# Expert stage of a transformer kernel: earlier first rows, later transposes of the picks, gates built for four tokens at a time

## What is computed

```python
def peer_ffn(h, w_q, sub_keys, u, v):           # h: 512 tokens x 1024
    q = (ht @ w_q).reshape(T, PEER_HEADS, 2, PEER_DKEY // 2)          # 8 heads
    s = jnp.einsum('thpc,hpnc->thpn', q, sub_keys, ...)               # 2 x 128 scores a head
    v1, i1 = lax.top_k(s[:, :, 0], K); v2, i2 = lax.top_k(s[:, :, 1], K)      # K = 16
    cand = (v1[..., :, None] + v2[..., None, :]).reshape(T, PEER_HEADS, K * K)
    cand_idx = (i1[..., :, None] * PEER_NKEYS + i2[..., None, :]).reshape(...)
    top_s, pos = lax.top_k(cand, K)
    idx = jnp.take_along_axis(cand_idx, pos, axis=-1)                 # 128 experts a token
    g = jax.nn.softmax(top_s, axis=-1)
    ...
        ue = jnp.take(u, ib, axis=0)                                  # u, v: 16384 x 1024, f32
        a = jnp.einsum('thkd,td->thk', ue, xb, ...)
        w = jax.nn.gelu(a) * gb
        ve = jnp.take(v, ib, axis=0)
        return jnp.einsum('thk,thkd->td', w.astype(ve.dtype), ve)
```

## Time and profile before

| | |
|---|---|
| median of the runs | 3234.04 us |
| the profiled execution's own time | 3241.02 us |
| its span in the profile | 3238.9 us |
| TensorE matmul, busy | 2821.2 us (87%) |
| VectorE, busy | 1888.5 us (58%) |
| ScalarE, busy | 709.6 us (22%) |
| GpSimd, busy | 767.5 us (24%) |
| HBM read | 538.52 MB |

### The profile page before, as it was taken

How to read it: one execution, slowest core, us unless ns; L and a number is a source line. 1 busy time by engine, 2 the same in 40 slices (tenths; PEclk the granted TensorE clock), 3 DMA queues, 4 the chain that set the end, 5 groups by cost and what they waited for, 6 DMA issues and landing times.

```text
span 3238.9 us, 29295 instructions
## 1 busy us (share of the span) xinstructions
PE 2821.2 (87%) x9642; PEld 1644.1 (51%) x9642; DVE 1888.5 (58%) x4008; ACT 709.6 (22%) x1851; POOL 767.5 (24%) x601
## 2 busy tenths in 40 slices
PE   9999999998889899988898998699888999999024
PEld 4455445454554444556645787588777444343012
DVE  4989502048760331257622569996776760687984
ACT  1114301022320112345411321122112100121222
POOL 0520100000000000013200444441110640576772
PEclk9999999999999999999999999799999999999557
DMA  4221112211011121000122798795444995999994
GB/s 182 78 97 60 65 56 100 78 52 52 27 66 52 71 89 55 27 27 27 53 95 101 288 380 319 255 323 165 146 142 142 388 406 180 410 409 410 356 347 151
DMA packets 125768, 544.49 MB, mean 168 GB/s; under 512 B 13888, under 2 KB 14272, under 8 KB 117568
## 3 DMA queue, kind: packets, MB, share of 16 engines
q0 software_dynamic: 73728, 268.47, 22.2%
q1 hardware_dynamic: 49472, 258.02, 21.6%
q10 hardware_dynamic: 2432, 16.29, 1.3%
HBM read 538.52 MB, written 4.19 MB: 168 GB/s over the span
## 4 chain that ended last, share of the span: by engine, by line
PE 57%; DMA 13%; DVE 12%; issue 8%; POOL 7%; ACT 2%; DVEq 0%; ACTq 0%; SPq 0%; POOLq 0%
PE ps L609 13%; PE ps L1135 9%; DMA ROW_U<-peer_u,C 7%; PE ps L724 6%; PE ps L661 4%; POOL ROW_U L1780 3%; POOL ROW_V L1789 3%; PE ps L954 3%; DMA ROW_V<-peer_v,C 2%; PE ps L862 2%; PE ps L983 2%; PE ps L891 2%; DMA STREAM<-experts 2%; PE ps L1060 2%; PE ps L1154 2%
## 5 line engine op out<-in xcount | busy, mean ns | idle before, releaser
L609 PE MATMUL ps<-XT,W 128*128 128x512 f32 (+1 forms) x1216 | 471.8, 548 | 6.8 <-issue 4.5
L1135 PE MATMUL ps<-XTD,STREAM 128*128 128x256 f32 x2048 | 467.5, 386 | 9.7 <-DMA STREAM<-experts 9.7
L1164 PE MATMUL ps<-STREAM,GD 128*128 128x512 f32 x1024 | 455.1, 602 | 15.7 <-DMA STREAM<-experts 14.1
L1135 PEld LDWEIGHTS ps<-XTD,STREAM 128*128 128x128 f32 x2048 | 390.8, 194 | 70.6 <-DMA STREAM<-experts 18.6
L1780 POOL DMA_INDIRECT ROW_U<-peer_u,C x226 | 291.1, 1288 | 497.1 <-DVE DOT L2435 461.4
L2447 DVE SCALAR_TENSOR_TENSOR X<-ROW_V,WEIGHT,X 128x1024 f32<-128x1024 f32 x226 | 290.2, 1284 | 170.0 <-issue 96.1
L609 PEld LDWEIGHTS ps<-XT,W 128*128 128x128 f32 x1216 | 229.6, 190 | 247.9 <-issue 238.4
L1164 PEld LDWEIGHTS ps<-STREAM,GD 128*128 128x128 f32 x1024 | 191.3, 191 | 277.6 <-issue 208.4
L1789 POOL DMA_INDIRECT ROW_V<-peer_v,C x226 | 264.7, 1171 | 220.3 <-DVE X L2447 168.8
L2435 DVE CUSTOM_DVE_ANT_0 ROW_U<-ROW_U,XN 128x1024 f32<-128x1024 f32 x226 | 275.4, 1219 | 48.3 <-DMA ROW_U<-peer_u,C 46.7
L724 PE MATMUL ps<-W,Y 128*128 128x512 f32 x512 | 226.1, 603 | 13.0 <-DVE Y L1951 6.1
(11 more groups left out here) (344 smaller groups left out, 3811.8 us busy)
## 6 DMA issues: line engine op xcount, KB each, us to landing
STREAM<-experts SPq DMA_DIRECT2D x256, 512.0 KB, 6.7
W<-wstream SPq DMA_DIRECT2D x53, 2048.0 KB, 8.1
GD<-wstream ACTq DMA_DIRECT2D x2, 2048.0 KB, 12.8
ROW_U<-peer_u,C POOLq DMA_INDIRECT x226, 8.8
ROW_V<-peer_v,C POOLq DMA_INDIRECT x226, 8.4
XT<-xT SPq DMA_DIRECT2D x8, 256.0 KB, 5.4
W<-wstream SPq DMA_DIRECT2D x8, 256.0 KB, 6.4
X<-x SPq DMA_DIRECT2D x1, 2048.0 KB, 19.6
```

What stands on the lines that cost most here:

```text
L609: mm = pe.matmul(b[:, 0:rhs[k].shape[-1]], w[:, k, m * P:(m + 1) * P], rhs[k], start=(k == 0), stop=(k == KD - 1))
L1135: mm = pe.matmul(UP_BANK[g % 2][:, 0:256], u[:, k, :], XTD[:, k, :], start=(k == 0), stop=(k == KD - 1))
L1164: mm = pe.matmul(acc(b, n)[:, :], GD[:, i * 256 + b * P:i * 256 + (b + 1) * P], STREAM[m % STREAM_RING][:, n * T:(n + 1) * T], start=(i == ...
```

## The change

The first rows are placed between VectorE's softmax of unit 0, the sums and factors of blocks 2 and 3, and the whole route of unit 1; ScalarE's roots and weights move with them. There are 48 early rows instead of 30, 46 rows ahead of the first pass instead of 34, and 106 by its end instead of 91. Unit 2 is routed ahead of block 2, unit 3 between block 2 and block 3. Block 2's exponentials, softmax end and transposes stand at steps 42, 43 and 45 instead of 32, 32 and 33; block 3's at 76, 77 and 79 instead of 68, 68 and 69. Gates are built from step 82 on, one or two quads of tokens a step, with both one-hot tiles of a quad from one VectorE instruction, the weights put in by four ScalarE copies, and three banks for the products instead of two. The loads for PLE and its wait stand 64 rows behind the loop instead of 30, and the first pieces of PLE 92 to 101 rows behind it instead of 70 to 82. In the diff a line in words after "..." says which engine's list follows.

```diff
-EARLY_ROWS = 30
+EARLY_ROWS = 48
...
-PICKED_2, PICKED_3 = 32, 68
+PICKED_2, PICKED_3 = 40, 74
+QUAD_FROM = 82
...
+def quads_by(g):
+    return max(0, min(64, (g - QUAD_FROM + 1) * 64 // (TILES - QUAD_FROM - 1)))
...
 def rows_by(g):
-        return 34
-    if g <= PICKED_3:
-        return 34 + (g + 1) * 5 // 8
-    return rows_by(PICKED_3) + (g - PICKED_3) // 4
+        return 46
+    if g <= QUAD_FROM:
+        return 46 + (g + 1) * 3 // 5
+    return rows_by(QUAD_FROM) + (g - QUAD_FROM) // 4
...
-ROUTE_ORDER = [("unit", 0), ("unit", 1), ("block", (2, 0)), ("block", (2, 1)), ("unit", 2), ("block", (2, 2)),
-               ("block", (2, 3)), ("block", (3, 0)), ("block", (3, 1)), ("unit", 3), ...
+ROUTE_ORDER = [("unit", 0), ("unit", 1), ("unit", 2), ("block", (2, 0)), ("block", (2, 1)), ("block", (2, 2)),
+               ("block", (2, 3)), ("unit", 3), ("block", (3, 0)), ("block", (3, 1)), ...
...
-        UP_BANK, BUILD_BANK, IT_BANK = (ps[0], ps[1]), (ps[2], ps[3]), ps[4]
+        UP_BANK, BUILD_BANK, IT_BANK = (ps[0], ps[1]), (ps[2], ps[3], ps[5]), ps[4]
...   TensorE, in step g
-                    if g == (PICKED_2, PICKED_3)[b - 2] + 1:
+                    if g == (PICKED_2, PICKED_3)[b - 2] + 5:
                         picks_transposed(b)
+            def build_quad(q):
+                pe.wait_ge(quad_scaled, q + 1)
+                if q >= 3:
+                    pe.wait_ge(quad_gated, q - 2)
+                for i in range(4):
+                    mm = pe.matmul(BUILD_BANK[q % 3][:, i * P:(i + 1) * P], ONE[q % 2][:, 1, i, :], ONE[q % 2][:, 0, i, :], ...
...   ScalarE
+            def scale_quad(q):
+                act.wait_ge(quad_hot, q + 1)
+                for i in range(4):
+                    ins = act.activation(ONE[q % 2][:, 1, i, :], ONE[q % 2][:, 1, i, :], ACT.Copy,
+                                         scale=IT[:, 2, 4 * q + i:4 * q + i + 1])
+                ins.then_inc(quad_scaled, 1)
...
             queries("wq0a", 0, (0, 1))
             block_copies("mT", 2)
             unit_exponentials(0)
+            row_roots(2)
             queries("wq1a", 1, (0, 1))
-            row_roots(2)
             rows_scaled(2)
             block_copies("mT", 3)
+            row_weights(4)
+            row_roots(3)
             queries("wq2a", 2, (0, 1))
-            row_roots(3)
             rows_scaled(3)
-            row_weights(3)
+            row_weights(8)
             queries("wq3a", 3, (0, 1))
-            row_weights(7)
+            row_weights(14)
             columns_gained(2)
             columns_gained(3)
-            row_weights(9)
             for q in range(4):
                 queries(f"wq{q}b", q, (2, 3))
-                row_weights(13 + 4 * q)
+                row_weights(20 + 6 * q)
...   ScalarE, in step g
-                    if g == at_step:
+                    if g == at_step + 2:
                         exponentials(b)
...
-                if r == rows_by(TILES - 1) + 30:
+                if r == rows_by(TILES - 1) + 64:
                     act.wait_ge(v_used, 68)
                     (five loads into GD: PLE_W, PROJ, PLE_P, XB)
-                if r == rows_by(TILES - 1) + 70:
+                if r == rows_by(TILES - 1) + 92:
                     ple_copies(0)
...   VectorE
             unit_softmax(0)
+            rows_to(1)
             row_factor(2)
+            rows_to(4)
+            while routed < 2:
+                draw_to(drawn + 1)
             residual_sum(3)
+            rows_to(6)
             row_factor(3)
-            for r in range(rows_by(-1)):
-                if r >= 6:
-                    draw_to(min(36 * 2, 36 + 3 * (r - 5)))
-                rows_to(r + 1)
+            rows_to(rows_by(-1))
...
+            def quad_ones(q):
+                if q % 32 == 0:
+                    dve.wait_ge(it_copied, q // 32 + 1)
+                if q >= 2:
+                    dve.wait_ge(built, q - 1)
+                wide = [P, 2, 4, P]
+                dve.tensor_tensor(ONE[q % 2][:, :, :, :], IOTA ... broadcast_to(wide), IT[:, 0:2, 4 * q:4 * q + 4] ..., ALU.is_equal)
...   VectorE, in step g
-                    if g == at_step:
+                    if g == at_step + 3:
                         soft_end(b)
...
+                for q in quads_of(g):
+                    quad_gates(q, g)
+                for q in quads_of(g + 1):
+                    quad_ones(q)
                 rows_to(rows_by(g))
```

More of the change, by code:

```diff
@@ L137 @@
 ROUTE_STEPS = 35
-ROUTE_ORDER = [("unit", 0), ("unit", 1), ("block", (2, 0)), ("block", (2, 1)), ("unit", 2), ("block", (2, 2)),
-               ("block", (2, 3)), ("block", (3, 0)), ("block", (3, 1)), ("unit", 3), ("block", (3, 2)), ("block", (3, 3)),
+ROUTE_ORDER = [("unit", 0), ("unit", 1), ("unit", 2), ("block", (2, 0)), ("block", (2, 1)), ("block", (2, 2)),
+               ("block", (2, 3)), ("unit", 3), ("block", (3, 0)), ("block", (3, 1)), ("block", (3, 2)), ("block", (3, 3)),
                ("unit", 4), ("unit", 5), ("unit", 6), ("unit", 7)]
@@ L478, in program @@
         it_copied = sem("it_copied")
-        pair_one1 = sem("pair_one1")
-        pair_one2 = sem("pair_one2")
+        quad_hot = sem("quad_hot")
+        quad_scaled = sem("quad_scaled")
         built = sem("built")
         gates_kept = sem("gates_kept")
-        pair_gated = sem("pair_gated")
+        quad_gated = sem("quad_gated")
         tile_gated = sem("tile_gated")
@@ L1145, in picks_transposed @@
                 mm.then_inc(it_full, 1)
-            def build_pair(p):
-                pe.wait_ge(pair_one1, p + 1)
-                pe.wait_ge(pair_one2, p + 1)
-                if p >= 2:
-                    pe.wait_ge(pair_gated, p - 1)
-                for i in range(2):
-                    mm = pe.matmul(BUILD_BANK[p % 2][:, i * P:(i + 1) * P], ONE_2[:, (2 * p + i) % 4, :],
-                                   ONE_1[:, (2 * p + i) % 4, :], start=True, stop=True)
+            def build_quad(q):
[3 more added lines that the diff above has]
+                for i in range(4):
+                    mm = pe.matmul(BUILD_BANK[q % 3][:, i * P:(i + 1) * P], ONE[q % 2][:, 1, i, :], ONE[q % 2][:, 0, i, :],
+                                   start=True, stop=True)
                 mm.then_inc(built, 1)
@@ L1210, in _ @@
                 for b in (2, 3):
-                    if g == (PICKED_2, PICKED_3)[b - 2] + 1:
+                    if g == (PICKED_2, PICKED_3)[b - 2] + 5:
                         picks_transposed(b)
-                for p in pairs_of(g):
-                    build_pair(p)
-            pe.wait_ge(pair_gated, TILES)
+                for q in quads_of(g):
+                    build_quad(q)
+            pe.wait_ge(quad_gated, 64)
             pe.wait_ge(tile_gated, sum(gated(g) > 0 for g in range(TILES)))
@@ L1694, in _ @@
                     at_step = (PICKED_2, PICKED_3)[b - 2]
-                    if g == at_step:
+                    if g == at_step + 2:
                         exponentials(b)
-                    if g == at_step + 2:
+                    if g == at_step + 6:
                         picks_copied(b)
-                for p in pairs_of(g):
-                    keep_pair(p, g)
+                for q in quads_of(g):
+                    keep_quad(q, g)
+                for q in quads_of(g + 1):
+                    scale_quad(q)
                 row_weights(rows_by(g) - LAG)
@@ L2506, in tile_gates, with quad_gates @@
+            def quad_gates(q, g):
+                dve.wait_ge(gates_kept, q + 1)
+                view = DENSE[:, 4 * q:4 * q + 4, 0:g + 1]
+                dve.tensor_tensor(view, view, BUILD_BANK[q % 3][:, :].rearrange("p (t i) -> p t i", t=4)[:, :, 0:g + 1],
+                                  ALU.mult).then_inc(quad_gated, 1)
             def tile_gates(g):
@@ L2553, in _ @@
                     tile_gates(g)
-                for p in pairs_of(g):
-                    pair_gates(p, g)
-                for p in pairs_of(g + 1):
-                    pair_hot(p)
+                for q in quads_of(g):
+                    quad_gates(q, g)
+                for q in quads_of(g + 1):
+                    quad_ones(q)
                 rows_to(rows_by(g))
@@ L2561, in _ @@
                 draw_to(12 * ROUTE_STEPS + 6 + (ROUTE_STEPS + 1) * (r - UNITS // 2 * UNIT_ROWS + 42) // UNIT_ROWS)
[L2562 removed]
+                if at_row == 92:
                     ple_scale(0)
[L2564 removed]
+                if at_row == 94:
                     ple_factor(0)
[L2566 removed]
+                if at_row == 101:
                     ple_out(0)
```

57 lines of the change are left out of this document (16 added, 41 removed).

## The result

The changed kernel takes 3112.34 us (median of 4 runs, 3110.21 to 3115.87) against 3233.7 us for the kernel before (4 runs, 3230.55 to 3244.62). The ratio is 0.962, 95% interval 0.9596 to 0.9644: 121 us less. The forecast was 3103, the range 3055 to 3150. The profiled execution took 3115.87 us, with a span of 3113.7.

A forecast was written before the change was run, and what follows sets the result against it. The rows were taken to set the end. Second pass from 2500 - 19 - 5 = 2476, plus 587 to the last addition, plus 44.7 tail and 2.1, 3110; against the median 3103, range 3055 to 3150.

The forecast's parts named there:

- The hole: Second pass, 2658 to 2746: VectorE, ScalarE and GpSimd idle; later PLE loads remove these 88 us, less 23 of DMA time.
- the hole comes back: Rival, chance 0.04: rows at 2.80 us reach row 170 before tile 68, 34 us of stop; 3128 us.
- 492 us at 3.85 give 128 more: Second pass: from 98 rows added at its start, 128 more at 3.85 us a row make 226.
- I add 5 us for it: TensorE's second pass: tiles that streamed through the idle stretch now share the DMA, 5 us more, 503.
- the mark of being wrong: Sign of a wrong forecast: rows during the second pass take more than 3.9 us, or that pass starts after 2500.
- E: Start of the second pass, forecast as 2500 - 19 - 5 = 2476; last addition at E + 587.
- Fifteen rows more: By the end of the first pass: 15 rows more done, at 2.8 us each 42 us.
- The front: Ahead of the first pass: VectorE's rows start earlier, 34 instead of 24 by 1885; 19 us gained by block 2's picks.
- The gates: Gate steps: TensorE waits 47 us instead of 52 on a 4.2 us chain, a gain of 5.
- TensorE runs through: Rival, chance 0.13: no stop at step 45, gate waits of 10; second pass from 2426, time 3053.
- The DMA at 344 GB/s: Rival, chance 0.03: from the second pass's start the DMA gives 344 GB/s, 689 us instead of 587; 3205.
- The granted clock: Rival "Slower", chance 0.03: many microsecond waits hold TensorE at 1.2 GHz through the gate steps, 213 us more, 3316.

The follow-up runs named there:

- 1: Kernel before with only the loads for PLE and their wait 64 rows, PLE's first pieces 92 to 101 rows, behind the loop: 3184.32 us, ratio 0.9841.
- 2: Changed kernel with only the loads and PLE's first pieces put back to 30 and 70 to 82 rows behind the loop: 3167.75 us, ratio 0.9786.
- 4: Changed kernel with the front of before, 34 rows ahead of the first pass: 3139.51 us, ratio 0.970.
- experiment 5: Changed kernel with VectorE's one-hot tiles for the next step's quads ahead of this step's gates: 3066.31 us, ratio 0.9478.
- 3: Changed kernel with gates for pairs of tokens and two banks as before, 128 pairs over the same 45 steps: 3165.24 us, ratio 0.9783.
- 8: Changed kernel with ScalarE copying a quad's other four one-hot tiles onto themselves ahead of its scaled copies: 3165.22 us, ratio 0.9775.

## Why the prediction was right

*The hole* (88 us gone, no wait at row 170, "the hole comes back" 0.04): right. The longest wait of ScalarE for a dot in the second pass is 12.2 us. Its price was the term that was mis-sized: 65 forecast, 55 and 59 measured (1, 2). The step that erred is "492 us at 3.85 give 128 more" together with "I add 5 us for it". The bytes give the length of the pass: 124 rows of 1.05 MB, 128 tiles of 0.52 and 7 of loads are 204 MB, at 400 GB/s 510 us (an estimate; the trace has 202.8 MB at 399 GB/s). The 3.85 held for windows of the kernel before, and the one behind the hole began with buffers that had filled during it, up to four u and four v rows, 4 MB (that this makes the difference is argued, no run shows it apart). So a row takes 4.0 us from the first addition on, above the 3.9 that I named as the mark of being wrong, 124 rows instead of 128 are added in the pass, and the pass takes 507.3 us instead of 503; from E to the last addition it is 593.5 against my 587. By that mark the step is wrong; the start of the pass, the other mark, came out.

*Fifteen rows more*: of 694.0 - 593.5 = 100.5 us, the hole takes 55 to 59, which leaves 42 to 46 for the rows, 15 x 2.8 = 42 forecast.

*The front*: first dot 1744.3 (1741 forecast), 33 dots by 1885 (34), third tile 8.1 us late (8), stop 10.7 (13), transposes 2079.6 (2079). Undoing it costs 26 us (4), where the forecast had 19 for front and later picks together. That the profile hit so well is partly luck, as that point moves by 10 us between executions.

*The gates*: right, by a chain that binds. One turn is 5.13 us; the forecast had 4.2 + 0.89 = 5.1. The waits are 48 us (259 - 211, experiment 5) against my 47. A scaled copy of SBUF data takes 386 ns, near the 0.4 us that I gave as the upper end, but one starts 0.29 us behind the other, and that is what the chain pays: four take 1.27 us in a row, where the four copies of PSUM data took 1.12. The Trainium skill (VectorE: DVE Perf Modes, section on the TRN2 errata) has it right: 0.17 us more a quad by the page, 0.15 here. The forecast's sum left it out, and its 0.5 for hand-overs proved wide enough to cover it: kept, gates, one-hot and copies come to 0.38 + 0.99 + 1.23 + 1.33 = 3.93 from start to start, and the build to 1.20 instead of 0.89.

*The second pass* starts at 2475.3, forecast 2476; the last addition ends at 3068.8, forecast 3063; median 3112, forecast 3103. Of the 9 us, 6.5 are the stretch behind E, and 3.5 that the profiled execution lies 3.5 above the median where the one of before lay 7 above it; E came 0.7 early.

*The rivals*: "TensorE runs through" is what experiment 5 made (no gate waits; E 2417 and 3066, where the rival had 2426 and 3053). The DMA at 344 GB/s didn't come: 399 over the whole pass. The Trainium skill's 358 GB/s of HBM per core (DMA: Bandwidth & Descriptors, Specifications) is passed here too, by this kernel on one core. The granted clock stayed at 0.99 in the gate steps with their many waits of about a microsecond; in 3, with waits of up to 4.1 us, it was 0.95, and in 8, with waits of up to 2.9, 0.96. The forecast's "only gaps of 4 us were followed by 4.94" was too narrow: in the changed kernel one tile takes 5.3 us behind a wait of 2.2 (at 2433.7), and in 8 six tiles take 4.2 to 5.8 behind waits of 2.1 to 2.9.
